# Mixer levels and softmax units interleaved on every engine, and 58 expert units instead of 56

## The chip, the cores and the metric

The kernel runs on one core of one Trainium2 chip. The metric is device time in microseconds (us); lower is better. Before the change three runs took 1692.69, 1696.32 and 1702.27 us, median 1696.32. The engines are named as in the profile: PE (TensorE, matmuls), DVE (VectorE), ACT (ScalarE), POOL (GpSimd) and SP (the queue that issues most loads).

## What is computed

One inference step of a two-layer trunk over 384 tokens (128 context, 256 latent; three tiles of 128), all in fp32, width 1024. Each layer has a modulated norm, one input projection, three mixers side by side (Fourier, differential attention, gated linear recurrence), an output projection, and a mixture of 64 experts with the best 8 for each token. Cut to the two mixers and the expert part that the change touches:

```python
# differential attention: 4 heads, two score maps a head
s = jnp.einsum('bqhmd,bkhmd->bmhqk', qblk, kf) * scale
p = jax.nn.softmax(s, axis=-1)
w = p[:, 0] - lam * p[:, 1]
o = jnp.einsum('bhqk,bkhd->bqhd', w, vf)

# recurrence (forward and backward), chunk by chunk
dec = jnp.where(causal, cum[:, :, :, None, :] - cum[:, :, None, :, :], -jnp.inf)
a = jnp.einsum('bhtk,bhsk,bhtsk->bhts', qc, kc, jnp.exp(dec))
o = o_inter + jnp.einsum('bhts,bhsv->bhtv', a, vc)

# experts: width 128, gates of the chosen 8
act = jax.nn.silu(hg) * hu * gates[:, :, None]
routed = jnp.einsum('tef,efd->td', act, p['w_down'])
```

## The kernel before

One program issues each engine's instructions in a fixed order written out by hand; the engines meet through semaphores. Within a layer the order is: modulation and norm, input projection (weights split into a high and a low part), Fourier mixer, recurrence, attention, output projection, router, experts, sum of the experts' rows.

**The recurrence in levels.** The pair matrix `aT` (source times target token, per tile and head) is filled by six levels (`NLEV`): four halvings of 64, 32, 16 and 8, and two last levels for the blocks of 8, forward and backward. For a level DVE takes differences of the summed log decays (`less_middle`, L1593, tile `diff` in `work`), ACT takes their exponentials (L1325, L1326; L1328, L1329 in the last two), DVE multiplies keys and queries with them (L1605, L1607; L1610, L1611), PE multiplies the two (L947, 12 products of 64 by 128, one for each tile, odd or even heads, and pair), and DVE copies the result under a mask into `aT` (`masked`, L1580). On DVE the products of level n come first, then the differences of n+1, then the masks of n-1. The levels' products go round all eight PSUM banks, six banks a level. After them: states (L957), the sum of the two halves of `aT` (L1624), the state copies, and the heads (L972, L976), which ACT takes out (L1336, L1337).

**The attention in units.** After the heads come twelve units, one for each tile and head, in a pipeline three deep on every engine. In step u, PE makes the two score maps of unit u (L990), turns the weights of unit u-2 (L998) and multiplies unit u-3 with the values (L1008); DVE takes the row maxima of unit u (L1646, L1648) and then makes the weights of unit u-1 (L1655 to L1660); ACT takes the exponentials of unit u (L1346), copies the turned weights of u-2 (L1353), and after a tile's last head copies the output and its squares (L1357, L1358). A unit of the first tile has 128 keys, the others 384. Scores and turned weights go round six banks, outputs use the other two. Then DVE sums the squares (L1670, L1671), ACT takes roots, DVE scales, and PE turns the rows (L1017). `prob`, `wts` and `wT` lie in the tile `h`, as do the sums `cum` and the keys `kkT` of the levels, so the attention can't start before the levels are done with them.

**Banks.** Every use of a bank is planned before: `banks.claim` makes PE wait until the use before it on the same bank was emptied, `banks.read` makes the reader wait until it was filled. A wait holds up all that stands behind it in its engine's order.

**Experts.** Tokens are packed into units of 128 rows, two windows of 64. A "whole" unit gives both windows to one of the busiest experts, a "pair" unit serves two experts, and a "spare" unit has windows for what overflows; the weights of a spare window are loaded only if it has an owner. With 56 units there are 16 whole, 24 pairs and 16 spare, in eight turns of "pair, whole, pair, spare, pair, whole, spare". Each load is one expert's 1.5 MB (3 x 512 KB). The 96 entries of the load list go round seven slots (`XSLOT`): SP waits for the unit that used the slot before, then issues; an entry without an owner keeps its slot. For each unit PE turns rows (L1129), makes gate and up products (L1143, 16 matmuls, 32 records), turns the activation (L1150) and makes the down products (L1158) of the unit before. POOL gathers and scatters the rows.

Of the kernel before, what the change touches and what calls it, by code (L numbers as in the profile page):

```python
# [18 lines left out]
ALU = mybir.AluOpType  # L19
# [3 lines left out]
P = 128  # L23
# [11 lines left out]
WIN = 64  # L35
NUNITS = 56
WHOLE = 16
PAIRED = 24
NXW = 32
# [110 lines left out]
def trunk_program(nc, T, CF, CM, y_prompt, y_sample, new_k, new_v, new_state):  # L150
# [22 lines left out]
    with ctx:  # L173
# [110 lines left out]
        prob = hflat[:, 0:4 * TOK].rearrange("p (a m t) -> p a m t", a=2, m=2)  # L284
        wts = hflat[:, 4 * TOK:6 * TOK].rearrange("p (a t) -> p a t", a=2)
        wT = hflat[:, 6 * TOK:8 * TOK].rearrange("p (a t) -> p a t", a=2)
        logf = mixer(NTILE, 2 * HW)
        att = logf
# [5 lines left out]
        att_sq = part(0, 4, DA)  # L294
# [86 lines left out]
        for stage, n in (("ada0", 2), ("ms1", 1), ("modT0", 2), ("ada1", 2), ("modT1", 2),  # L381
                         ("ada2", 2), ("q", DH), ("k", DH), ("modT2", 2), ("v", NTILE), ("fn", NTILE), ("hq", 2),
                         ("hif", NTILE), ("hbg", NTILE), ("k_rows", 1), ("ckT", 1), ("rotq", 2), ("rotk", 2),
                         ("four1", 4), ("zT", 2), ("fnT", 2), ("kkT", 4), ("cum", 4), ("past", 2), ("ada3", 2)):
            banks.plan("layer", stage, n)
        for use in range(2 * NTILE * NLEV):
            if use == 2 * NTILE:
                banks.plan("layer", "modT3", 2)
            banks.plan_one("layer", "lev", use, banks.turn % 8)
            banks.turn += 1  # L390
        for stage, n in (("st", 2), ("ho", 2)):
            banks.plan("layer", stage, n)
        UNITS = [(t, hd) for t in range(NTILE) for hd in range(DH)]
        NU = len(UNITS)
        ring6 = 0
        for u in range(NU + 3):
            if u < NU:
                for m in range(2):
                    banks.plan_one("layer", "sc", 2 * u + m, ring6 % 6)
                    ring6 += 1  # L400
            if 2 <= u < NU + 2:
                banks.plan_one("layer", "wT", u - 2, ring6 % 6)
                ring6 += 1
            if u >= 3 and UNITS[u - 3][1] == 0:
                banks.plan_one("layer", "o", UNITS[u - 3][0], 6 + UNITS[u - 3][0] % 2)
# [122 lines left out]
        for turn in range(8):  # L528
            for kind in ("pair", "whole", "pair", "spare", "pair", "whole", "spare"):
                u = UNITS_BY_KIND[kind].pop(0)  # L530
                owners = {"whole": [u], "pair": [u, u + PAIRED], "spare": [E + u - WHOLE - PAIRED, E + u - WHOLE - PAIRED + 16]}[kind]
                loads_of_unit.append([len(loads) + i for i in range(len(owners))] * (2 if kind == "whole" else 1))
                loads += [(len(order_of_units), w) for w in owners]
                order_of_units.append(u)
# [209 lines left out]
        def _(pe):  # L744
# [21 lines left out]
            for l in range(DEPTH):  # L766
# [169 lines left out]
                for n in range(NLEV):  # L936
                    if n == 1:
                        modulation_turned(3)
                    ka, qa = key_side[:, n % 2, :, :], query_side[:, n % 2, :, :]
                    pe.wait_ge(pair_ready.sem, pair_ready.at(l, n + 1))  # L940
                    for t in range(NTILE):
                        for odd in range(2):
                            use = (n * NTILE + t) * 2 + odd
                            bk = banks.claim(pe, "lev", use)
                            r = slice(HK * odd, HK * (odd + 1))
                            for c in range(2):
                                last = mm(bk[:, c * P:(c + 1) * P], ka[r, c, t * P:(t + 1) * P],  # L947
                                          qa[r, c, t * P:(t + 1) * P], start=True, stop=True)
                            banks.filled(last, "lev", use)


                pe.wait_ge(kdec_ready.sem, kdec_ready.at(l, 1))
                for i, tiles in enumerate(((0, 0), (1, 2))):
                    bk = banks.claim(pe, "st", i)
                    for d, t in enumerate(tiles):
                        for a in range(2):
                            last = mm(bk[:, (2 * d + a) * P:(2 * d + a + 1) * P], kdec[:, 2 * i + d, a * P:(a + 1) * P],  # L957
                                      hv[:, t, a * P:(a + 1) * P], start=True, stop=True)
# [992 lines left out]
```

## Time and profile before

| | us |
|---|---|
| runs, median of 3 | 1696.32 |
| profiled execution, its own time | 1706.42 |
| its span in the profile | 1704.6 |
| PE busy | 1406.1 (82%) |
| DVE busy | 671.4 (39%) |
| ACT busy | 408.3 (24%) |
| POOL busy | 256.3 (15%) |
| mean granted clock of PE | 0.881 |

The profile is that of one execution. Busy time is that of instructions of an engine; a share is over the whole span, whose stages have different limits. The granted clock is 1.0 at 2.4 GHz and 0.5 at 1.2 GHz; a stretch between them is a mix. Rows of a timeline give the start in us, the time taken in us, the engine and line, the operation, what it writes and reads, the number of instructions, and in brackets the idle time before it with what ended that. PE writes two records for each fp32 matmul.

### The profile page before, as it was taken

What the parts mean: (1) busy time and instruction counts of PE and PEld (TensorE: products, weight loads), DVE (VectorE), ACT (ScalarE), POOL (GpSimd) and SP (SyncE); (2) the same over time, 40 slices, a digit from 0 to 9 for tenths busy, and PEclk for the clock granted to TensorE, in tenths of its full rate; (3) what the DMA queues carried; (4) which work ended last, traced back from release to release, by engine and by line L of the source; (5) the groups of instructions that cost most, each with busy time, mean ns of one, the idle gap of its engine ahead of it and who ended that gap; (6) DMA issues with size and microseconds to landing.
All of it is one profiled execution on the core that took longest, in us unless ns stands there. A gap on an engine that the chain in (4) does not pass through costs nothing.

```text
span 1704.6 us, 23713 instructions
## 1 busy us (share of the span) xinstructions
PE 1406.1 (82%) x8772; PEld 962.6 (56%) x8772; DVE 671.4 (39%) x1382; ACT 408.3 (24%) x788; POOL 256.3 (15%) x273
## 2 busy tenths in 40 slices
PE   4799687986999999997059996888889999999942
PEld 2598465954555555554028875676655555555521
DVE  4422767153332222222743347633523222222246
ACT  2324425021222222221013344321112122222201
POOL 1000000001322222231010000000023232322200
PEclk9799857977999999999579996699889999999975
DMA  9553202126988888885874412122469888888853
GB/s 319 206 183 118 105 31 109 50 87 233 362 305 317 328 333 324 305 332 181 340 257 173 141 70 99 41 99 99 180 252 358 333 313 307 324 294 298 328 207 154
DMA packets 126098, 378.96 MB, mean 222 GB/s; under 512 B 28224, under 2 KB 33152, under 8 KB 122784
## 3 DMA queue, kind: packets, MB, share of 16 engines
q1 hardware_dynamic: 86976, 291.31, 46.2%
q0 software_dynamic: 35552, 60.97, 10.1%
q10 hardware_dynamic: 3456, 25.17, 3.6%
q8 instruction: 71, 1.16, 0.3%
q14 instruction: 43, 0.35, 0.1%
HBM read 480.36 MB, written 64.75 MB: 320 GB/s over the span
## 4 chain that ended last, share of the span: by engine, by line
PE 71%; DVE 16%; DMA 6%; issue 4%; ACT 2%; SPq 0%; DVEq 0%; ACTq 0%; POOLq 0%
PE bank L1143 25%; PE bank L1158 11%; PE bank L1129 7%; PE bank L1050 5%; PE bank L771 4%; PE bank L772 4%; PE bank L773 4%; DVE aT L1843 4%; DMA ring<-in_w_ada 3%; DVE aT L1580 1%; PE bank L1066 1%; DMA ring<-in_w_in 1%; PE bank L790 1%; PE bank L1114 1%; PE bank L976 1%
## 5 line engine op out<-in xcount | busy, mean ns | idle before, releaser
L1143 PE MATMUL bank<-slab,xT 128*64 128x256 f32 x2112 | 301.5, 396 | 20.6 <-issue 20.5
L1143 PEld LDWEIGHTS bank<-slab,xT 128*64 128x64 f32 x2112 | 180.6, 142 | 104.2 <-issue 38.2
L732 POOL DMA_INDIRECT sums_scratch<-h,row_table x112 | 112.8, 1007 | 538.6 <-PE bank L1129 438.4
L1826 DVE TENSOR_TENSOR work<-work,bank 128x128 f32<-128x128 f32 x112 | 32.3, 288 | 399.1 <-ACT work L1405 399.1
L1143 PE MATMUL bank<-ring,xT 128*64 128x256 f32 x960 | 152.7, 392 | 9.6 <-issue 9.6
L1158 PE MATMUL bank<-slab,work 128*64 128x512 f32 x528 | 147.3, 592 | 1.5 <-DVE work L1832 1.5
L1405 ACT ACTIVATE work<-bank 128x128 f32<-128x128 f32 x112 | 31.1, 278 | 457.5 <-PE bank L1143 457.5
L1815 DVE COPY h<-bank 128x512 f32<-128x512 f32 x112 | 77.5, 692 | 127.0 <-PE bank L1158 127.0
L1143 PEld LDWEIGHTS bank<-ring,xT 128*64 128x64 f32 x960 | 90.1, 140 | 44.8 <-issue 14.8
L1143 PE MATMUL bank<-h_hi_slot,xT 128*64 128x256 f32 x512 | 108.5, 396 | 6.4 <-issue 6.4
L1492 DVE TENSOR_TENSOR w_lo<-ring,w_hi 128x2048 fp32r<-128x2048 f32 x24 | 55.0, 2292 | 122.3 <-ACT w_hi L1229 122.3
L1129 PEld LDWEIGHTS bank<-consts,big 128*128 128x128 f32 x544 | 60.8, 145 | 68.3 <-issue 51.7
L1809 DVE COPY xT<-bank 128x512 f32<-128x512 f32 x112 | 77.5, 692 | 54.7 <-PE bank L1129 54.5
L1392 ACT ACTIVATE xT<-bank 128x512 f32<-128x512 f32 x112 | 67.1, 599 | 114.6 <-PE bank L1129 114.6
L1129 PE MATMUL bank<-consts,big 128*128 128x128 f32 x544 | 77.7, 288 | 16.0 <-DMA big<-rows_scratch,token_table 16.0
L1050 PE MATMUL bank<-big,ring 128*128 128x384 f32 x256 | 84.9, 488 | 0.0
L1179 PE MATMUL bank<-consts,aT 128*128 128x128 f32 x48 | 11.8, 428 | 88.4 <-DVEq L1846 88.4
L1398 ACT ACTIVATE h<-bank 128x512 f32<-128x512 f32 x112 | 67.0, 598 | 68.5 <-PE bank L1158 68.5
L725 POOL DMA_INDIRECT big<-rows_scratch,token_table x68 | 69.1, 1017 | 90.5 <-DVE token_table L1799 64.8
L1050 PEld LDWEIGHTS bank<-big,ring 128*128 128x128 f32 x256 | 80.1, 314 | 3.7 <-DVE mod L1464 0.2
L790 PE MATMUL bank<-ring,scond_wide 128*32 128x512 f32 x384 | 56.4, 724 | 29.8 <-DMA ring<-in_w_ada 29.8
L1229 ACT ACTIVATE w_hi<-ring 128x2048 fp32r<-128x2048 f32 x24 | 46.0, 1916 | 142.6 <-PE bank L773 87.6
(334 smaller groups left out, 2324.9 us busy)
## 6 DMA issues: line engine op xcount, KB each, us to landing
slab<-in_w_gate SPq DMA_DIRECT2D x112, 512.0 KB
slab<-in_w_up SPq DMA_DIRECT2D x112, 512.0 KB
slab<-in_w_down SPq DMA_DIRECT2D x112, 512.0 KB
ring<-in_w_ada SPq DMA_DIRECT2D x24, 2048.0 KB
ring<-in_w_gate SPq DMA_DIRECT2D x52, 512.0 KB
ring<-in_w_up SPq DMA_DIRECT2D x52, 512.0 KB
ring<-in_w_down SPq DMA_DIRECT2D x52, 512.0 KB
slab<-sums_scratch ACTq DMA_DIRECT2D x24, 1024.0 KB, 11.5
```

Source lines behind the costliest of these rows:

```text
L725: pool.indirect_dma_start(x_slots[n % XBUF], None, rows_dram, bass.IndirectOffsetOnAxis(ap=token_table[:, u:u + 1], axis=0), bounds_check= ...
L732: pool.indirect_dma_start(sums_dram, bass.IndirectOffsetOnAxis(ap=row_table[:, u:u + 1], axis=0), y_rows[:, n % 3, :], None, bounds_check= ...
L771: mm(out, a[0], b[0], start=start, stop=False)
L772: mm(out, a[0], b[1], start=False, stop=False)
L773: return mm(out, a[1], b[0], start=False, stop=stop)
L790: last = mm(bk[GROUP * ji:GROUP * (ji + 1), :], scond_wide[:, 4 * half + ji, :], w[:, ji, c * 512:(c + 1) * 512], start=(half == 0), stop= ...
L1050: last = mm(bk[:, 0:TOK], w[:, c, j:D:NJ], mixT[:, 4 * half + c, :], start=(half == 0 and c == 0), stop=(half == 1 and c == 3))
L1129: last = tr(bk[:, j * P:(j + 1) * P], x_slots[n % XBUF][:, (4 * half + j) * P:(4 * half + j + 1) * P], ident)
L1143: last = mm(bk[r, 0:2 * P].rearrange("p (k f) -> p k f", k=2), xT[:, n % 2, j, r], w[:, j, :, :], start=(j == 0), stop=(j == NJ - 1))
L1158: last = mm(bk[r, :], actT[:, n % 2, r], expert_slot(n, half)[0][:, 2 * D + c * 512:2 * D + (c + 1) * 512], start=True, stop=True)
L1809: banks.emptied(copy(xT[:, n % 2, 4:8, :].rearrange("p j s -> p (j s)"), bk[:, :]), "XTb")
L1815: banks.emptied(copy(y_rows[:, n % 3, 512:1024], bk[:, :]), "Yb")
```

## The change

The change does three things.

- **Order.** A list `STEPS` names levels, mask steps, units, states and heads in one order, and PE, ACT and DVE each run through it. Level 0 and its masks come first; from level 1 on there are two units to a level, one after `level` and one after `masks`; states, heads of tile 0, 1 and 2 are put between units 9 to 13. A level goes over PE in two parts: `level(n, 0)` covers tiles 0 and 1, `level(n, 1)`, in the mask step, covers tile 2. DVE does the second part's masks of level n-1 at the end of the level step, and the first part's masks of level n in the mask step.
- **Banks and memory.** Levels, states and heads have banks 6 and 7; scores 0 to 3; turned weights 4; outputs 5. `prob`, `wts` and `wT` move from `h` to the memory of `h_hi`, `att` and one tile of squares to that of `xT`. ACT sums each head's squares with `accum_out`, four instructions for each tile, and DVE's reduction of the attention's squares (L1670) goes.
- **Experts.** 58 units: 14 whole, 25 pairs, 19 spare; the load list has 102 entries. The order begins with "pair, whole, pair, pair, spare, pair" and is then dealt in proportion; the last is a spare. Written P, W, s it is: P W P P s P s W s W P s P W s P P s W P s W P s P P W s P s W P P s W P s P W s P P s W P s P W P s P W s P W s P s.

The diff, cut to its core:

```diff
-NUNITS = 56
-WHOLE = 16
-PAIRED = 24
-NXW = 32
+NUNITS = 58
+WHOLE = 14
+PAIRED = 25
+SPARE = NUNITS - WHOLE - PAIRED
+NXW = 2 * SPARE
...
-        prob = hflat[:, 0:4 * TOK].rearrange("p (a m t) -> p a m t", a=2, m=2)
+        prob = h_hi_slot[:, 0:4 * TOK].rearrange("p (a m t) -> p a m t", a=2, m=2)
...
-        att = logf
+        x_flat = xT[:, :, :, :].rearrange("p a j s -> p (a j s)")
+        att = x_flat[:, 0:NTILE * DA].rearrange("p (i f) -> p i f", i=NTILE)
+        att_sq = x_flat[:, NTILE * DA:NTILE * DA + DA]
...
+        banks.plan("layer", "ada3", 2, [0, 1])
+        banks.plan("layer", "modT3", 2, [2, 3])
+        banks.plan("layer", "lev", 4 * NLEV, [6, 7] * (2 * NLEV))
+        banks.plan("layer", "st", 2, [6, 7])
+        banks.plan("layer", "ho", 2, [6, 7])
...
+                    banks.plan_one("layer", "sc", 2 * u + m, 2 * (u % 2) + m)
...
+        LEVEL_PARTS = [((0, 1), 0), ((0, 1), 1), ((2,), 0), ((2,), 1)]
+        STEPS = [("level", 0), ("masks", 0), ("level", 1), ("unit", 0), ("masks", 1), ("unit", 1), ("level", 2), ("unit", 2),
+                 ("masks", 2), ("unit", 3), ("level", 3), ("unit", 4), ("masks", 3), ("unit", 5), ("level", 4), ("unit", 6),
+                 ("masks", 4), ("unit", 7), ("level", 5), ("unit", 8), ("masks", 5), ("unit", 9),
+                 ("states", 0), ("unit", 10), ("heads", 0), ("unit", 11), ("heads", 1), ("unit", 12), ("heads", 2),
+                 ("unit", 13), ("unit", 14)]
...
+        kinds = ["pair", "whole", "pair", "pair", "spare", "pair"]
+        total = {kind: len(units) for kind, units in UNITS_BY_KIND.items()}
+        while len(kinds) < NUNITS - 1:
+            late = {k: (total[k] - (k == "spare")) * (len(kinds) + 1) / (NUNITS - 1) - kinds.count(k) for k in total}
+            kinds.append(max((k for k in total if k != "spare" or kinds[-1] != k), key=late.get))
...
+                def level(n, part):
+
                     ka, qa = key_side[:, n % 2, :, :], query_side[:, n % 2, :, :]
                     pe.wait_ge(pair_ready.sem, pair_ready.at(l, n + 1))
...
+                    for k in (2 * part, 2 * part + 1):
+                        tiles, odd = LEVEL_PARTS[k]
+                        bk = banks.claim(pe, "lev", 4 * n + k)
+                        r = slice(HK * odd, HK * (odd + 1))
+                        for i, t in enumerate(tiles):
                             for c in range(2):
...
+                for what, k in STEPS:
+                    if what == "level":
+                        level(k, 0)
+                    elif what == "masks":
+                        level(k, 1)
+                        if k == 0:
+                            modulation_turned(3)
+                    elif what == "unit":
+                        unit(k)
+                    elif what == "states":
+                        states()
+                    else:
+                        heads(k)
...
+                        for hd in range(DH):
+                            cols = slice(hd * P, (hd + 1) * P)
+                            last = af(att_sq[:, cols], bk[:, cols], ACT.Square, accum_out=att_r[:, 0, t * DH + hd:t * DH + hd + 1])
+                        banks.emptied(last, "o", t)
...
+                for what, k in STEPS:
+                    if what == "level":
+                        level(k)
+                        if k == 0:
+                            rows_of_modulation(3)
+                    elif what == "unit":
+                        unit(k)
+                    elif what == "heads" and k == NTILE - 1:
+                        heads_taken()
...
+                        masked(n - 1, 1)
...
+                less_middle(0)
+                for what, k in STEPS:
+                    if what == "level":
+                        level(k)
+                    elif what == "masks":
+                        masked(k, 0)
+                        if k == 0:
+                            modulation(3)
+                    elif what == "unit":
+                        unit(k)
+                    elif what == "states":
+                        states()
...
-                red(att_r[:, 0, :], heads_a(att_sq), AX.X, ALU.add)
```

## Rows read from the trace of the kernel before

**Rows 1.** The head of the page.
```profile
span 1704.6 us, 23713 instructions
```

**Rows 2.** Busy time by stretch, all engines, granted clock, DMA share, GB/s.
```profile
195.00:236.00 41.00, 25.62 (x168) 22.52 (x168) 36.79 (x76) 11.41 (x22) 0.76 (x1) 0.54 0.23 92
236.00:251.00 15.00, 14.49 (x65) 12.80 (x66) 0.68 (x3) 1.29 (x4) 0.15 (x1) 0.56 0.04 9
251.00:283.00 32.00, 26.17 (x130) 17.14 (x131) 25.14 (x83) 19.37 (x67) 1.46 (x3) 0.73 0.14 50
404.00:805.00 401.00, 372.15 (x2744) 219.06 (x2744) 110.58 (x233) 82.63 (x168) 112.86 (x112) 0.97 0.82 301
1031.00:1072.00 41.00, 25.72 (x168) 22.61 (x168) 36.80 (x76) 11.41 (x22) 0.71 (x1) 0.54 0.23 92
```

**Rows 3.** The chain of waits, expert units of layer 0: start, us, what.
```profile
464.90 3.60 PE bank L1143 x32
...
474.86 6.21 PE bank L1143 x32
483.93 3.60 PE bank L1143 x32
490.38 3.60 PE bank L1143 x32
```

**Rows 4.** One expert unit's stretch: PE busy, clock, DMA share, GB/s.
```profile
459.65:466.10 6.45, 6.45 (x53) 1.00 1.03 413
```

**Rows 5.** The page's DMA queue of SP: packets, MB, share.
```profile
q1 hardware_dynamic: 86976, 291.31, 46.2%
```

**Rows 6.** Timeline of DVE, levels of layer 0.
```profile
195.29 1.82 DVE L1593 TENSOR_TENSOR work<-h 128x768 f32<-128x768 f32 x2
...
198.94 0.56 DVE L1605 TENSOR_TENSOR work<-h,work 128x384 f32<-128x384 f32 x1 [1.83 <-ACT work L1326]
...
208.42 2.09 DVE L1580 COPY_PREDICATED aT<-masks,bank 128x256 f32<-128x256 uint8 x6
...
232.30 1.76 DVE L1624 TENSOR_TENSOR aT<-aT 128x1536 f32<-128x1536 f32 x1
```

**Rows 7.** Timeline of DVE, the start of two attention units.
```profile
265.55 1.02 DVE L1646 TENSOR_REDUCE top<-bank 128x1 f32<-128x384 f32 x2
...
268.07 1.01 DVE L1646 TENSOR_REDUCE top<-bank 128x1 f32<-128x384 f32 x2
```

**Rows 8.** Timeline of ACT, one attention unit.
```profile
264.24 0.58 ACT L1346 ACTIVATE h<-bank,ntop 128x384 f32<-128x384 f32 x1 [1.30 <-DVE ntop L1648]
...
265.37 0.49 ACT L1353 ACTIVATE h<-bank 128x384 f32<-128x384 f32 x1
```

**Rows 9.** Timeline of PE, parts of attention units.
```profile
258.59 1.65 PE L990 MATMUL bank<-slab 64*128 64x384 f32 x4
...
263.02 0.87 PE L998 MATMUL bank<-consts,h 128*128 128x128 f32 x3
...
269.42 0.92 PE L990 MATMUL bank<-slab 64*128 64x384 f32 x4
...
278.77 1.49 PE L1008 MATMUL bank<-slab,h 128*128 128x128 f32 x6
...
280.69 2.16 PE L1008 MATMUL bank<-slab,h 128*128 128x128 f32 x12
```

**Rows 10.** Timeline of PE, the last level and the states.
```profile
228.18 3.09 PE L947 MATMUL bank<-work 64*128 64x128 f32 x24 [0.97 <-DVE work L1611]
231.20 3.50 PE L957 MATMUL bank<-slab 128*128 128x128 f32 x16
```

**Rows 11.** Timeline of PE, two quarters of the heads.
```profile
238.00 0.69 PE L972 MATMUL bank<-slab,aT 128*128 128x64 f32 x2
...
239.67 0.69 PE L972 MATMUL bank<-slab,aT 128*128 128x64 f32 x2
```

**Rows 12.** Timeline of DVE, the attention's squares.
```profile
284.16 1.75 DVE L1670 TENSOR_REDUCE att_r<-work 128x12 f32<-128x1536 f32 x1 [4.48 <-ACT work L1358]
```

More of the change, by code:

```diff
@@ L293, in trunk_program @@
         four1 = part(0, 4)
-        att_sq = part(0, 4, DA)
         zT = part(4, 6)
@@ L946, in _ @@
                             for c in range(2):
-                                last = mm(bk[:, c * P:(c + 1) * P], ka[r, c, t * P:(t + 1) * P],
+                                last = mm(bk[:, (2 * i + c) * P:(2 * i + c + 1) * P], ka[r, c, t * P:(t + 1) * P],
                                           qa[r, c, t * P:(t + 1) * P], start=True, stop=True)
[L949 to L958, printed above, removed]
-                    banks.filled(last, "st", i)
@@ new lines, in heads @@
+                def heads(t):
+                    if t == 0:
+                        pe.wait_ge(qdec_ready.sem, qdec_ready.at(l, 1))
+                        pe.wait_ge(pairs_summed.sem, pairs_summed.at(l, 1))
+                        banks.wait_emptied(pe, "st", 1)
+                    for odd in range(2):
+                        if t == 0:
+                            banks.claim(pe, "ho", odd)
+                        bk = banks.banks[banks.uses["layer"]["ho", odd][0]]
+                        r = slice(HK * odd, HK * (odd + 1))
@@ L977, in _, with unit @@
                                               start=False, stop=(d == 1))
-                    banks.filled(last, "ho", odd)
-                pe.wait_ge(rope_done.sem, rope_done.at(l, 1))
-                banks.wait_emptied(pe, "ckT")
-                for u in range(NU + 3):
+                        if t == NTILE - 1:
+                            banks.filled(last, "ho", odd)
+                def unit(u):
+                    if u == 0:
+                        pe.wait_ge(rope_done.sem, rope_done.at(l, 1))
+                        banks.wait_emptied(pe, "ckT")
                     if u < NU:
@@ L1312, in _, with level @@
                 af(lam_s[:, :], lam_s[:, :], ACT.Exp).then_inc(lam_exp.sem, 1)
-                for n in range(NLEV):
-                    if n == 2:
-                        rows_of_modulation(3)
+                def level(n):
                     act_e.wait_ge(diff_ready.sem, diff_ready.at(l, n + 1))
@@ L1594, in less_middle, with level @@
                     last.then_inc(diff_ready.sem, 1)
-                less_middle(0)
-                for n in range(NLEV):
+                def level(n):
                     dve.wait_ge(fac_ready.sem, fac_ready.at(l, n + 1))
```

136 lines of the change are left out of this document (60 added, 76 removed).

## Prediction

> **What bounds the kernel now.** I read the page's head first [rows 1]: the profiled execution spans 1704.6 us and took 1706.4, 10 above the median of 1696.3, so the sum is made as a difference and added to both. Then the table of stretches [rows 2]. The reader is to see two different limits. In the mixer levels (195 to 236 us, and 1031 to 1072 in the second layer) DVE is busy 36.8 of 41 us and PE runs at a granted 0.54. In the heads of the mixer (236 to 251) DVE has nothing: 0.68 of 15. In the attention (251 to 283) DVE is busy 25.1 of 32. In the expert loop PE is busy 372 of 401. The part that the change interleaves goes from the first difference at 195.3 to the end of the last attention product at 280.69 + 2.16 = 282.85 [rows 6, 9]: 87.5 us, of which DVE is idle some 25. That idle time is the most that interleaving can win in a layer; the expert units are a separate matter.
>
> **Part 1: two more expert units.** The chain of waits shows a unit every 6.45 us: 483.93 to 490.38 [rows 3]. Two more, in two layers, are 4 x 6.45 = 25.8 us if nothing gives way. Something may: in each turn of seven units one waits for its weights, here from 471.4 to 474.86, and its matmuls take 6.21 instead of 3.60 at a lower clock. From 464.90 to 483.93 two units took 19.03 instead of 12.9, so 6.1 were lost. I walked the old load list by the code's rule (load i waits until the unit of load i-7 is done, skipped spare loads hold a slot all the same): the waits fall on units 9, 16, 23, 30, 37, 44, 51, the third unit of a turn, and 9 is where the trace has it. The bound is the slots, not the DMA engines, which carry 413 GB/s in one stretch of 6.45 us [rows 4] and 301 over the loop. No spare load ran before: the 291.31 MB of the queue [rows 5] are the dense weights and 128 experts. The new list still has 64 real loads, but puts two pairs side by side. The same walk gives it waits at units 5, 16, 25, 32, 41 and 48: six, not seven, four of them 1.5 us longer (two pairs after each other need four loads in 12.9 us). 4 x 1.5 more and one wait of about 3.7 less: about nothing, or 2 us less for shorter slow spells. So 11 to 13 us a layer; I take 12, **+24 us in all**, with 16 and 32 as ends. The wider one-hot tables (58 columns for 56) cost under 0.1 us on DVE and I count nothing.
>
> **Part 2: the interleaving.** What each engine does stays nearly the same; the order changes, and with it the handoffs. Durations before: on DVE a level is four products (198.94 to 200.9, 1.95 us), two differences (1.83) and six masked copies (2.09, 0.35 each) [rows 6]; a wait of 1.83 for ACT's exponentials shows what those take; the sum of the masks is done at 232.30 + 1.76 = 234.1. Old order: the masks of level n-1 cover the exponentials of n+1, and eight banks let PE run ahead. A later softmax unit costs 2.52 us on DVE (265.55 to 268.07) [rows 7]; a unit of the first tile, with a third of the keys, I put at 1.6 (an estimate). On ACT it is two exponentials (0.58) and a copy (0.49, of which 0.4 until the next can start) [rows 8]. On PE its scores take 1.65 us at the half clock and 0.92 at full, its transposes 0.87, its product 1.49 (1.3 to the next start) [rows 9]. A level's 24 matmul records take 3.09 at the half clock; the states take 3.50 [rows 10].
>
> New order, walked through the list of steps. The levels have two banks, so a level goes over PE in two parts: 16 records (3.09 x 16/24 = 2.1 us), and 8 (1.1). A part can't start before DVE has emptied both banks, and PE takes steps in order, so the scores of the next unit stand queued behind that part. Three handoffs follow, each on the path.
> (a) Level, then unit. DVE ends its level step with the last two masked copies of the level before. Only then does PE start the first part, 2.1, and then the scores, 1.65. The two halves of the rows overlap by some 0.45 (an estimate: the 24 records of rows 10, 0.43 us each, fit into 3.09 because both halves run together), and DVE waits 3.3 us; 2.5 for the first tile, whose scores are a third as wide. Twice 2.5 and three times 3.3 (levels 1 to 5): 14.9.
> (b) Masks, then unit. The second part and the scores: 1.1 + 1.65 - 0.65 = 2.1 (the first bank is free one mask earlier); 1.4 for the first tile. Two and three of these: 9.1.
> (c) Unit, then level. ACT takes the exponentials of the level in the same place of the list, behind those of the unit: 1.15 + 0.4 + 1.8, while DVE has 1.4 us of its own: 1.9 us of waiting, 1.6 for the first tile. Levels 2 to 5: 7.3.
> At the start DVE waits 1.8 for the first exponentials, and for the rows of modulation 3, which PE turns after the second part of level 0: 0.3 + 3.0. In total 36.4 us of waits. To them come DVE's own works up to the sum of the masks: 34.5 of the levels (36.8 less the 2.3 of the states) and 20 of the units 0 to 9 (four at 1.6, six at 2.52, less the last half). Together 90.9, where the trace has 234.1 - 195.3 = 38.8.
>
> **The end of it.** From there PE is the bound, at the half clock: wait for the states 1.5; units 10 and 11 at 1.65 + 0.87 + 1.3 = 3.8 each; heads of tile 0, 1.0; heads of tiles 1 and 2, each 4 x 1.66 = 6.64 (239.67 less 238.00 is one of four quarters [rows 11]); after each the transposes and product of an old unit, 2.2; last product 1.5. Sum 29.3. So the last attention product ends 90.9 + 29.3 = 120.2 us after the start, against 87.5: **+32.7 a layer**. Heads and units of PE don't overlap, they follow each other, and the idle time of DVE under the heads comes back at another place. The squares of the attention are now summed on ACT: DVE's reduction of 1.75 us goes [rows 12], ACT takes four small squares instead of one large, about 0.8 more: -1.0 a layer, on the path to the norm. The walk in the old order, with the same durations, ends at 284.8 where the trace has 282.8, so it is good to some 2 us in 88. The moved tiles (probabilities and attention rows in free memory) add no wait that I find. SP's and POOL's queues keep their order: the shared expert's weights wait for the heads, and the weight blocks of the next modulation for PE, 32 us later but with the same time ahead of them. **+31.7 x 2 = +63**.
>
> **The clock.** PE idles 5 and 2.5 us in each cycle of the new order and is busy for about 60% of it, as in the old levels (25.6 of 41), which ran at 0.54 [rows 2]. So I take half rate. In the last 29 us PE is nearly without a gap; there the old heads, busy 14.5 of 15 us, had 0.56, but the attention after them rose to full during the second tile. The Trainium skill, TensorE: Matmul & The Clock Gate, Part 1: The HAM clock gate, says that the default state is throttled and that sustained activity releases it; by that alone the end would run at 2.4 GHz, and the sum would be 4 to 6 us less a layer. The trace speaks against it for the heads. I keep half rate and put full rate into the range.
>
> **Sum.** +24 + 63 = +87. 1706.4 + 87 = 1793 for an execution like the profiled one, **1783 us** against the median.
>
> **Rivals.**
> R1, PE granted the full clock (17%). Then (a) becomes 1.2 + 0.92 - 0.4 = 1.7 and (b) 1.2, waits fall by some 13 us, and the end from 29.3 to 23.4: +13 a layer, 26 + 24 = +50, **1746**. For it: attention at full rate from 265 us. Against: the gaps.
> R2, it becomes faster (7%). PE's products for DVE are always there, and DVE is the bound: 62.2 us of work from rows 2, start 1.8, modulation 3.3 and 5 of drain = 72 against 87.5, -16.5 a layer with the saved reduction: -33 + 24 = -9, **1687**, -0.5%. It decides if (a) and (b) stay under 0.3 us each. Against: four banks for the scores don't help when they are queued behind a blocked level part.
> R3, the new spare units are free (8%), because they fill the waits for loads: +63 alone, **1759**. Against: two units add slots' worth of time only where there is a wait, and the pairs side by side eat that.
> R4, the interleaving does nothing (8%): waits won under the heads equal those lost: +24, **1720**.
> R5, about nil by half of R2's gain (5%): **1698**.
> My forecast: 55%, its own range 1768 to 1800.
>
> **How the numbers follow.** Faster by over 0.5% (8.5 us, about what a measurement of this kernel can tell): R2, 0.07. Within: R5, 0.05. Slower: 0.88. The range reaches from R1 and below it (some full clock with cheap units) to the forecast with dearer loads: 1728 to 1806; R2, R4 and R5 stay out.
>
> **What would show it.** In the profile after: DVE's reductions of a unit waiting for PE's scores, 2 to 3 us, behind each level and each mask step; level products waiting for ACT near 1.9; the sum of the masks about 91 us behind the first difference and the last attention product about 120; granted clock near 0.55; 58 units of 6.45 and six or so waits. If the sum of the masks comes within 70, R2's side is right, and the place of PE's scores in the queue was read wrongly.

## The result and the profile after

The changed kernel takes **1813.09 us**, median of three runs (1812.61 to 1814.11), against 1696.32 before: ratio **1.0685** [1.0635, 1.0734], +116.8 us. The direction was forecast; the time lies 30 us above the predicted 1783 and 7 above the range. The head of the page of the changed kernel, its shares of busy time and SP's queue (packets, MB, share), which answer to [rows 1] and [rows 5]:

```profile
span 1812.3 us, 24367 instructions
...
PE 1456.2 (80%) x8968; PEld 1001.7 (55%) x8968; DVE 679.4 (37%) x1396; ACT 416.3 (23%) x842; POOL 263.6 (15%) x281
...
q1 hardware_dynamic: 86976, 291.31, 43.5%
```

The loads are the same to the byte. This execution took 1814.11 us and stands 1 us above its median, where the profiled one of before stood 10 above its own. So two traces put side by side show 107.7 us, and the medians 116.8.

Where they went, by stretches cut at the same instructions in both traces (us; layer 0 / layer 1):

| stretch | before | after |
|---|---|---|
| first difference to first matmul of the output projection ("mixer") | 101.2 / 98.9 | 132.4 / 133.7 |
| output projection to the router's table | 105.5 / 104.7 | 106.2 / 105.3 |
| table to the first gate/up matmul | 12.4 / 11.8 | 13.8 / 13.6 |
| first to last gate/up matmul ("loop") | 382.3 / 386.0 | 404.1 / 402.2 |
| last gate/up matmul to the new x | 61.5 / 52.7 | 60.9 / 53.2 |

The mixers take 66.0 us of the 107.7, the loops 38.0, the table's way to the experts 3.2. Nothing else moved by more than 0.7.

Windows of the changed kernel (bounds, length, busy time of PE, PEld, DVE, ACT, POOL, granted clock, DMA share, GB/s), to be read against [rows 2]:

```profile
195.00:290.00 95.00, 51.08 (x252) 41.19 (x254) 56.10 (x139) 25.24 (x79) 0.00 (x0) 0.57 0.10 40
290.00:316.00 26.00, 23.92 (x118) 19.08 (x122) 8.12 (x23) 9.01 (x35) 2.37 (x4) 0.68 0.16 53
447.00:849.00 402.00, 377.04 (x2787) 223.32 (x2787) 111.42 (x236) 83.14 (x170) 107.84 (x107) 0.97 0.79 288
1085.00:1179.00 94.00, 49.73 (x239) 39.87 (x240) 55.08 (x138) 25.24 (x79) 0.00 (x0) 0.55 0.11 42
```

In the first and the last row no engine is busy for even 60% of the time: DVE has 56 of 95 us, PE 51, ACT 25. Before, DVE had 36.8 of 41 in the levels. So in the interleaved stretch no engine is the bound; they wait for each other. The timeline of DVE shows how (start, us, line, operation, and in brackets the idle time before it and its releaser):

```profile
258.55 0.76 DVE L1624 COPY_PREDICATED aT<-masks,bank 128x256 f32<-128x256 uint8 x2
262.82 1.25 DVE L1686 TENSOR_REDUCE top<-bank 128x1 f32<-128x384 f32 x2 [3.51 <-PE bank L1005]
...
265.57 1.42 DVE L1624 COPY_PREDICATED aT<-masks,bank 128x256 f32<-128x256 uint8 x4
268.98 1.16 DVE L1686 TENSOR_REDUCE top<-bank 128x1 f32<-128x384 f32 x2 [1.99 <-PE bank L1005]
...
273.63 0.96 DVE L1654 TENSOR_TENSOR work<-slab,work 128x768 f32<-128x768 f32 x1 [1.91 <-ACT work L1358]
...
288.15 1.76 DVE L1669 TENSOR_TENSOR aT<-aT 128x1536 f32<-128x1536 f32 x1
...
316.10 0.95 DVE L1724 TENSOR_REDUCE ho_r<-big 128x12 f32<-128x768 f32 x1 [16.97 <-ACT xT L1391]
```

One cycle has the three handoffs of the prediction (each is a wait of one engine for what another has to finish first): after the level's masks 3.51 us for the scores, after the next masks 1.99 for the scores, then 1.91 for ACT's exponentials. The sum of the masks starts at 288.15, 93.0 us after the first difference (37.0 before [rows 6]). The last row is DVE idle for 16.97 us under the heads and the last units: the idle time of the heads has moved, not gone. PE in the same cycle, and at the end:

```profile
259.13 2.42 PE L955 MATMUL bank<-work 64*128 64x128 f32 x13 [6.34 <-DVE aT L1624]
261.14 1.00 PE L1005 MATMUL bank<-slab 64*128 64x384 f32 x1
261.35 0.84 PE L955 MATMUL bank<-work 64*128 64x128 f32 x3
261.94 1.53 PE L1005 MATMUL bank<-slab 64*128 64x384 f32 x3
...
266.48 1.36 PE L955 MATMUL bank<-work 64*128 64x128 f32 x6 [1.75 <-DVE aT L1624]
...
297.26 0.33 PE L985 MATMUL bank<-slab,aT 128*128 128x64 f32 x2
...
298.11 0.43 PE L985 MATMUL bank<-slab,aT 128*128 128x64 f32 x2
...
309.13 0.69 PE L985 MATMUL bank<-slab,aT 128*128 128x64 f32 x2
...
311.49 2.76 PE L1024 MATMUL bank<-slab,h_hi_slot 128*128 128x128 f32 x12
```

PE stands idle for 6.34 us although the scores of the next unit (L1005) have all they need: they are queued behind the level's products (L955), which wait for DVE's masks. The last attention product ends at 314.25, 119.1 us after the start.

In the expert loop, PE's waits (total, number, longest), of the kernel before from 415 to 800 us and of the changed one from 447 to 850:

```profile
PE bank L1143 <- issue: 18.2, 7, 3.5
```
```profile
PE bank L1173 <- issue: 25.0, 10, 5.3
```

Seven waits for weights became ten. The chain of waits of the changed kernel shows the longest, at unit 16 of layer 0 (start, us, what):

```profile
545.41 3.60 PE bank L1173 x32
551.86 5.34 issue
557.20 6.01 PE bank L1173 x32
566.06 3.60 PE bank L1173 x32
572.51 3.60 PE bank L1173 x32
```

The wait costs 5.34, and the unit's products run 6.01 instead of 3.60, so the next one starts 2.4 us late too. Without waits a unit starts 6.45 us behind the one before. In layer 0 the starts lie further apart at units 5 (by 1.8), 16 (5.4), 19 (1.5), 25 (3.2), 28 (1.0), 32 (4.0), 35 (1.4), 41 (3.1), 44 (1.5) and 48 (2.9), and at the unit right behind five of them (by 1.7 to 2.3).

### The profile page after: what moved, and what is told of

It is laid out like the page before. It is cut to its first block, busy times and chain, and to the rows that moved or that the text cites. A ratio compares the mean times of both kernels' runs of the same rounds, so it can differ in the third digit from the quotient of the medians.

```text
span 1812.3 us, 24367 instructions
## 1 busy us (share of the span) xinstructions
PE 1456.2 (80%) x8968; PEld 1001.7 (55%) x8968; DVE 679.4 (37%) x1396; ACT 416.3 (23%) x842; POOL 263.6 (15%) x281
## 4 chain that ended last, share of the span: by engine, by line
PE 72%; DVE 14%; DMA 6%; issue 4%; ACT 3%; SPq 0%; DVEq 0%; POOL 0%; POOLq 0%; ACTq 0%
PE bank L1173 24%; PE bank L1188 11%; PE bank L1159 7%; PE bank L1080 5%; PE bank L780 4%; PE bank L782 4%; PE bank L781 4%; DVE aT L1896 3%; PE bank L955 3%; DMA ring<-in_w_ada 3%; PE bank L1005 1%; PE bank L1096 1%; DMA ring<-in_w_in 1%; PE bank L799 1%; DMA big<-rows_scratch,token_table 1%
## 5 line engine op out<-in xcount | busy, mean ns | idle before, releaser
L1173 PE MATMUL bank<-slab,xT 128*64 128x256 f32 x2016 | 260.9, 404 | 43.5 <-issue 43.5
L1173 PEld LDWEIGHTS bank<-slab,xT 128*64 128x64 f32 x2016 | 161.8, 145 | 124.5 <-issue 60.5
L1173 PE MATMUL bank<-ring,xT 128*64 128x256 f32 x992 | 124.9, 382 | 5.7 <-issue 5.7
L955 PE MATMUL bank<-work 64*128 64x128 f32 x288 | 57.8, 433 | 86.7 <-DVE aT L1624 72.9
L1188 PE MATMUL bank<-slab,work 128*64 128x512 f32 x504 | 124.7, 593 | 1.5 <-DVE work L1885 1.5
L955 PEld LDWEIGHTS bank<-work 64*128 64x128 f32 x288 | 51.4, 315 | 94.7 <-issue 69.7
L1173 PE MATMUL bank<-h_hi_slot,xT 128*64 128x256 f32 x704 | 102.8, 382 | 0.2 <-issue 0.2
L1862 DVE COPY xT<-bank 128x512 f32<-128x512 f32 x116 | 80.2, 691 | 59.4 <-PE bank L1159 59.1
L1159 PE MATMUL bank<-consts,big 128*128 128x128 f32 x576 | 82.2, 288 | 19.2 <-DMA big<-rows_scratch,token_table 19.2
L1173 PEld LDWEIGHTS bank<-ring,xT 128*64 128x64 f32 x992 | 76.1, 137 | 37.3 <-issue 10.6
L734 POOL DMA_INDIRECT big<-rows_scratch,token_table x72 | 73.0, 1014 | 92.0 <-DVE token_table L1852 63.1
L1209 PE MATMUL bank<-consts,aT 128*128 128x128 f32 x48 | 11.8, 426 | 88.3 <-DVEq L1899 88.3
```

Of the source, the lines that this page charges most:

```text
L734: pool.indirect_dma_start(x_slots[n % XBUF], None, rows_dram, bass.IndirectOffsetOnAxis(ap=token_table[:, u:u + 1], axis=0), bounds_check= ...
L955: last = mm(bk[:, (2 * i + c) * P:(2 * i + c + 1) * P], ka[r, c, t * P:(t + 1) * P], qa[r, c, t * P:(t + 1) * P], start=True, stop=True)
L1159: last = tr(bk[:, j * P:(j + 1) * P], x_slots[n % XBUF][:, (4 * half + j) * P:(4 * half + j + 1) * P], ident)
L1173: last = mm(bk[r, 0:2 * P].rearrange("p (k f) -> p k f", k=2), xT[:, n % 2, j, r], w[:, j, :, :], start=(j == 0), stop=(j == NJ - 1))
L1188: last = mm(bk[r, :], actT[:, n % 2, r], expert_slot(n, half)[0][:, 2 * D + c * 512:2 * D + (c + 1) * 512], start=True, stop=True)
L1862: banks.emptied(copy(xT[:, n % 2, 4:8, :].rearrange("p j s -> p (j s)"), bk[:, :]), "XTb")
```

## The experiments

**Theory.** The mixers lose time because PE and ACT take their steps in DVE's order: work that is ready stands behind work that waits for DVE. The loops lose it to the two units and to the *order* of the load list. **Rivals:** the clock, PSUM banks or DVE's own instructions in the mixers; in the loops the mere number of spare entries, or the rate of the DMA engines. All kernels were measured beside the kernel before. In the table the mixer and loop columns are from one trace each.

| kernel | ratio [95%] | median us | masks' sum starts after | mixer L0 / L1 | loop L0 / L1 |
|---|---|---|---|---|---|
| after | 1.0685 [1.0635, 1.0734] | 1813.1 | 93.0 | 132.4 / 133.7 | 404.1 / 402.2 |
| units58 | 1.0306 [1.0257, 1.0355] | 1747.3 | 37.0 | 100.5 / 101.1 | 404.0 / 403.7 |
| mix56 | 1.0316 [1.0265, 1.0368] | 1754.8 | 92.3 | 131.9 / 131.1 | 385.7 / 381.3 |
| mix56_scores | 1.0194 [1.0143, 1.0246] | 1730.1 | 74.4 | 115.9 / 115.9 | 371.9 / 382.1 |
| mix56_act | 1.0278 [1.0242, 1.0314] | 1748.0 | 85.9 | 127.0 / 126.7 | 384.1 / 379.5 |
| mix56_both | 1.0060 [1.0029, 1.0090] | 1705.9 | 65.2 | 106.7 / 107.5 | 382.9 / 382.0 |
| mix56_more | 0.9991 [0.9969, 1.0014] | 1695.9 | 65.4 | 101.8 / 101.2 | 376.9 / 377.3 |
| dealt56 | 0.9964 [0.9938, 0.9990] | 1690.4 | 37.0 | 101.1 / 100.5 | 380.2 / 378.1 |
| walk56 | 0.9984 [0.9958, 1.0009] | 1693.9 | 37.0 | 101.0 / 98.9 | 387.4 / 376.8 |
| walk58 | 1.0073 [1.0049, 1.0096] | 1706.4 | 37.0 | 100.5 / 98.9 | 381.2 / 387.0 |
| heads | 0.9913 [0.9884, 0.9941] | 1684.1 | 37.0 | 94.7 / 95.0 | 386.2 / 381.2 |
| heads_dealt56 | 0.9909 [0.9884, 0.9934] | 1682.4 | 37.0 | 94.7 / 96.9 | 381.5 / 377.6 |

### The two halves of the change apart

**units58** is the kernel before with the units and their order of the change; **mix56** is the changed kernel with the 56 units of before, so its edit is the reverse of that of units58, which is:

```diff
-NUNITS = 56
-WHOLE = 16
-PAIRED = 24
+NUNITS = 58
+WHOLE = 14
+PAIRED = 25
...
-        for turn in range(8):
-            for kind in ("pair", "whole", "pair", "spare", "pair", "whole", "spare"):
+        kinds = ["pair", "whole", "pair", "pair", "spare", "pair"]
...
```

> The kernel before with the change's expert part alone: 58 units (14 whole, 25 pairs, 19 spare) in the new order; mixers and attention as before. My forecast had +24 us. The theory after the result (the new load order adds small waits at units 19, 28, 35 and 44 that my walk with shorter load times did not show, and the seven real loads at the start delay the first gather) says +41: 38 in the two loops and 3 before them. If the expert loop costs more only because it follows the new mixers, this run stays near +24.

> The change's interleaving alone, with the 56 units, their counts and their order as before. My forecast had +63; the two traces put +66 on this part. If both parts are independent, the excess of this run and that of units58 add up to that of the changed kernel, 107 to 117.

units58 cost +3.06%, mix56 +3.16%; together 6.2, the change 6.85 [6.35, 7.34]. In medians it is 51.9 and 59.4 us, together 111, within the 107 to 117 expected. Each half is known to 0.5%, so within the noise they add up, and neither hides the other. The loops of units58 (404.0, 403.7) are those of the changed kernel, and its mixers are those of before. By medians units58 is +52 us, where the theory said 41 and the forecast 24. By loops it is less: fourteen loops of the old order, from this table and the kernel before, lie between 371.9 and 386.2 with a mean of 381.4; four of the new one between 402.2 and 404.1, mean 403.5. That is **+22 a layer**, of which two units of 6.45 are 12.9. PE's waits in one loop of units58, from 430 to 850 us:

```profile
PE bank L1149 <- issue: 25.0, 10, 4.6
```

Ten waits again. mix56 has DVE's waits of the changed kernel to within 0.5 us: 24.2 for the scores there, the other three rows alike (from 194 to 320 us: total, number, longest):

```profile
DVE top L1681 <- PE bank L1000: 23.7, 12, 3.5
...
DVE work L1644 <- ACT work L1350: 5.0, 3, 1.8
DVE work L1649 <- ACT work L1353: 3.6, 2, 1.9
DVE mod L1503 <- PE bank L808: 3.0, 2, 2.4
```

### PE: the scores ahead of what waits for DVE

In **mix56_scores** PE issues the scores of a unit ahead of the level part, states or heads that stand in front of it. No instruction is added.

```diff
-                for what, k in STEPS:
+                for at, (what, k) in enumerate(STEPS):
+                    if what == "unit":
+                        if STEPS[at - 1][0] == "unit":
+                            scores(k)
+                    elif STEPS[at + 1][0] == "unit":
+                        scores(STEPS[at + 1][1])
```

> As mix56, but PE issues the scores of the next unit ahead of the level part (or states, or heads) that stands before that unit in the list; nothing else moves, no work is added or removed. Theory one (the handoff: scores queued behind a level part that waits for DVE's masks): DVE's waits of 3.5 and 2.0 us for scores go, 19 us a layer, so about 38 us less than mix56. Theory two (PE's total work at the half clock is the bound, wherever it stands): within 6 us of mix56.

```profile
DVE mod L1511 <- PE bank L808: 6.2, 4, 2.5
DVE top L1689 <- PE bank L1000: 5.1, 4, 1.9
DVE work L1652 <- ACT work L1358: 5.0, 3, 1.8
DVE work L1657 <- ACT work L1361: 3.6, 2, 1.9
DVE aT L1627 <- PE bank L950: 2.7, 6, 1.4
```

The wait for the scores falls from 23.7 to 5.1 us, the sum of the masks starts 17.9 earlier, and the mixers lose 16.0 and 15.2, together 31; the medians differ by 25. Expected were 38. The masks now wait a little for their own products (2.7 instead of 0.5), as they should when the scores go first. (Two of the four waits for the modulation belong to the next stage, which now lies in the window; in the levels they are 2.36 and 0.66 as before.) The granted clock rose too, from 0.56 to 0.64 (195.6 to 271), so a faster PE is a rival. The first part of the stretch tells them apart, since it ran at the half clock throughout (a stretch with its clock of 0.50, and the last reduction of the first tile):

```profile
197.60:231.50 33.90, 20.41 (x104) 17.60 (x104) 22.83 (x61) 10.75 (x35) 0.00 (x0) 0.50 0.22 87
```
```profile
228.69 0.49 DVE L1689 TENSOR_REDUCE top<-bank 128x1 f32<-128x128 f32 x2 [0.35 <-PE bank L1000]
```

There the four reductions of the first tile wait 0.35 us in all instead of 8.6 in the changed kernel, and the last of them starts 33.1 us after the first difference instead of 39.7: the same matmuls in another order do that without the clock. In the rest of the stretch, at 0.74, what the order gives and what the clock gives aren't told apart.

### ACT: the exponentials ahead of the unit's

**mix56_act** lets ACT take the exponentials of levels 2 to 5 one step earlier; **mix56_both** is that on top of mix56_scores.

```diff
+                act_steps = list(STEPS)
+                for n in range(2, NLEV):
+                    at = act_steps.index(("level", n))
+                    act_steps.insert(at - 1, act_steps.pop(at))
-                for what, k in STEPS:
+                for what, k in act_steps:
```

> As mix56, but ACT takes the exponentials of levels 2 to 5 one unit earlier; PE's order stays the change's. Theory one (each handoff is a wait of its own on DVE's path, so they add): 8 us a layer less than mix56, 16 in all, as between mix56_scores and mix56_both. If the wait for ACT is only the shadow of the wait for PE, it gives nothing without the other edit.

> As mix56_scores, and ACT takes the exponentials of levels 2 to 5 one unit earlier in its order. Theory one: the waits of 1.6 to 1.9 us of DVE for ACT at four levels go, 8 us a layer, so about 54 us less than mix56, and still some 10 us above the kernel before, because the end of the mixers (states, heads, last units) stays PE's. Theory two: within 10 us of mix56.

DVE's waits, of mix56_act and then of mix56_both:

```profile
DVE top L1685 <- PE bank L1000: 24.2, 11, 3.5
...
DVE work L1648 <- ACT work L1350: 1.8, 1, 1.8
```
```profile
DVE top L1693 <- PE bank L1000: 3.1, 3, 1.6
DVE aT L1631 <- PE bank L950: 2.7, 6, 1.4
DVE work L1656 <- ACT work L1358: 1.8, 1, 1.8
```

In both only the first level's exponentials are still waited for; the four later waits, 6.8 us, are gone. Alone this gives 4.9 and 4.4 us a mixer, less than the 8 that I expected: the sum of the masks comes 6.4 earlier, but the end is PE's and gives 1.5 of it back. On top of the scores it gives 9.2 and 8.4, and the median of mix56_both is 49 us below that of mix56, of 54 expected. So the two waits shadow each other a little, and together they carry **25.2 and 23.6 of the 30.7 and 32.2 us** that interleaving had cost: (a) to (c) were the main cause. The banks and DVE's own instructions are the same in mix56_both as in mix56, so these two rivals have at most the 5.5 and 8.6 us that are left. mix56_both is still 0.6% slower than before, with a sum of the masks at 65.2.

### What is left: heads in pairs, modulation later

**mix56_more** adds two things: it puts the products of odd and even heads of the same tile next to each other, and lets modulation 3 come one step later on PE and DVE. **heads** is the first of these alone, on the kernel before.

```diff
-                    bk = banks.claim(pe, "ho", odd)
-                    r = slice(HK * odd, HK * (odd + 1))
-                    for t in range(NTILE):
-                        for c in range(2):
+                    banks.claim(pe, "ho", odd)
...
+                for t in range(NTILE):
...
+                    for c in range(2):
+                        for odd in range(2):
...
+                        if t > 0:
+                            for d in range(2):
+                                src = state0 if (t == 1) == (d == 0) else st_mid
+                                for odd in range(2):
+                                    r = slice(HK * odd, HK * (odd + 1))
+                                    last[odd] = mm(outs[odd][c], qdec[r, 2 * d + c, t * P:(t + 1) * P], src[r, 2 * d + c, :],
+                                                   start=False, stop=(d == 1))
```

> As mix56_both, with the heads' products grouped as in the run heads, and modulation 3 turned on PE after the first part of level 1 and taken by DVE ahead of the masks of level 1. Expected: 5 us a layer less for the heads and 2 to 3 us for modulation 3, for which DVE waited 2.4 us in level 0: about 15 us less than mix56_both, the mixers at 99 us a layer against 101 before: near the kernel before, within 0.5%. If PE's work at half the clock is by now the bound of the whole stretch, only the heads' 5 us a layer come.

> The kernel before, with the products of the mixer's heads in another order on PE: for each tile and pair, the products of odd and even heads stand next to each other (two banks, two halves of the rows), so that the products with 64 rows can run side by side. Same products, nothing added. Theory one (a quarter of 1.66 us is four 64-row records after each other and two changes between 128 and 64 rows): 3.3 us less a layer, 6 to 7 in all. Theory two (weight loads or the granted clock of about 0.55 set the pace of the heads): no change. In either case the whole time lies under 0.5% from before, so the trace's heads stretch decides.

The timeline of PE in heads, one pair of quarters, where [rows 11] had two of 1.67 one after the other:

```profile
238.47 1.11 PE L973 MATMUL bank<-slab,aT 128*128 128x64 f32 x4
239.51 0.69 PE L980 MATMUL bank<-state,big 64*128 64x64 f32 x4
240.00 0.64 PE L980 MATMUL bank<-st_mid,big 64*128 64x64 f32 x4
240.57 1.11 PE L973 MATMUL bank<-slab,aT 128*128 128x64 f32 x4
```

A pair takes 2.10 us, against 2 x 1.67 = 3.34. The products over 128 rows cost a little less (1.04 to the next start for four records, where two had 0.62): 0.2 of the 1.24 us. Those over 64 rows, one head on rows 0 to 63 and the other on 64 to 127, now start 0.49 and 0.57 us apart for four records, as before for two: they run side by side, which is the other 1.04. The records are as long as before (0.69, 0.64), at a granted 0.57 against 0.56, so it isn't the clock. The Trainium skill, TensorE: Matmul & The Clock Gate, Part 3: Packing small matmuls, says that products with few rows run at the same time when they lie in different row groups of the array; the trace agrees, for fp32 and two groups. heads gained 0.87% [0.59, 1.16], more than the 0.5% expected, with mixers 6.5 and 3.9 us shorter; the four pairs of a layer make 5.0. The mixers of mix56_more are 4.9 and 6.3 shorter than those of mix56_both, and its median is 10 us lower, of 15 expected. The later modulation has no share in this that shows: the sum of the masks starts no earlier (65.4 after 65.2), since the wait only moved and grew (3.0 to 4.0 together):

```profile
212.10 0.19 DVE L1519 TENSOR_REDUCE mod<-bank 128x8 f32<-128x32 f32 x1 [3.38 <-PE bank L808]
212.95 0.19 DVE L1519 TENSOR_REDUCE mod<-bank 128x8 f32<-128x32 f32 x1 [0.66 <-PE bank L808]
```

With all of it, interleaving has a mixer of 101.5 where the order of before, with heads in pairs, has 95. On this kernel it doesn't pay even when its handoffs are mended.

### The order of the load list

Three orders, each a string of P (pair), W (whole) and s (spare), in the diff in this order. **dealt56**: the kernel before, its own 16, 24 and 16 units dealt by the rule of the change. **walk56** and **walk58**: orders that a walk of the load list rated best, with one fixed time for a load; walk58 has the 14, 25 and 19 units of the change.

```diff
-        for turn in range(8):
-            for kind in ("pair", "whole", "pair", "spare", "pair", "whole", "spare"):
+        for kind in 'PWPPsPWsWsPWPsPWsPWPsPWsPWPsPWPsWPsPWPsWPsPWPsWPPsWPsWPs':
+        for kind in 'PWPPPsWPsWPWsPPsWPsPWWsPPsPsWPWsPPWWsPPsWPsPWWsPPWWsPPss':
+        for kind in 'PPPWPWsPPssPsPWsWWPsPWPsPWWsPPsPsWPsPsWPWsPPsWPWsPsPsWPsPs':
```

> The kernel before (56 units, its counts, its mixers), with its units in the order that the change's dealing rule gives for them: P W P P s P W s W s P W P s P W s and so on. Theory S (the waits come from which unit frees a slot for which load, so the order of the units sets them, and the number of units costs 6.45 us each): my walk of the load list gives 10 us less a layer than the old order, so about 20 us less than before. Theory D (the DMA engines are the bound of the loop, order does not matter): within 5 us of before.

> As dealt56, with an order chosen by walking the load list so that few units wait: P W P P P s W P s W P W s P P s W P s P W W s P P s P s W P W s P P W W s P P s W P s P W W s P P W W s P P s s. Theory S: 20 to 26 us less a layer than the old order, 40 to 50 us less than before in all. Theory D: within 5 us of before.

> The kernel before with the change's counts (58 units: 14, 25, 19), in an order walked in the same way. Theory S: two units more cost 12.9 us a layer but the waits fall by more, so 5 us less a layer than the kernel before, about 10 less in all, and some 55 us less than units58, which has the same counts. If the number of units, or the larger tables, were the cost: near units58, 40 to 50 above before.

(In the order of the change as it is written out ahead of the prediction, units 21 and 22 are exchanged: the rule deals a pair and then a whole.) dealt56 was expected 20 us faster and gave 6 (0.36%, [0.10, 0.62]). walk56 was expected 40 or more faster and gave nothing that can be measured; in its layer 0 the starts lie too far apart at units 7 (2.1 us), 14 (4.3), 17 (3.2), 33 (3.2) and 41 (3.8), among others. So the walk with one fixed load time rates orders wrongly, and that theory fell. These two runs alone would fit the rival, the rate of the DMA engines, nearly as well: it said within 5 us of before. walk58 decides. It was expected 10 us faster than before and took 9 to 12 more (1.0073), but against units58, with the same units, spare entries and loads in another order, it is 1706.4 to 1747.3. So neither the number of spare entries nor the engines' rate alone sets the time of units58. PE's waits of walk58 from 415 to 800 us, and its busy row from 414.5 to 795.5:

```profile
PE bank L1144 <- issue: 10.6, 6, 3.3
```
```profile
414.50:795.50 381.00, 370.42 (x2807) 218.40 (x2805) 110.97 (x235) 82.92 (x170) 108.80 (x108) 1.00 0.82 301
```

Six waits of 10.6 us instead of ten of 25.0, and the granted clock rounds to 1.00 for the stretch: one unit is slow behind a wait, unit 11 with 5.36. The engines moved 301 GB/s, where the loop of the change had 288. With 58 units the two loops take 384.1 in the mean, 2.7 more than with 56; the order of the change makes that 22.1. **The two more units cost some 3 us a layer in a good order; the order of the change costs the other 19.** The 3 is rough: it rests on loops of 381.2 and 387.0, and by the medians the whole kernel is 9 to 12 us slower than before, 4 to 6 a layer. Each unit still takes its 6.45; what walk58 saves is waits. Which property makes an order good stays open: not the number of waits that my walk counts.

### A kernel faster than both

**heads_dealt56** joins heads and dealt56, with the edits shown.

> The two edits that gained, together, on the kernel before: heads grouped, and its 56 units in the order of dealt56. They touch different stages, so the gains should add: 0.87% and 0.36%, together 1.2%, about 1677 us; faster than both kernels.

0.9909 [0.9884, 0.9934], 1682.4 us, where 1677 was expected: faster than both kernels, by the paired heads. What dealt56 had shown, 6 us, doesn't show on top of heads' 0.9913; loops of one order spread by up to 14 us, and 6 us is near what can be told.

## Why the prediction was right, and where it failed

**Part 2, the interleaving: right, with two misses that cancel.** Forecast +31.7 a layer; the traces show +31.2 and +34.8 (the mixers of before differ by 2.3 between the layers, those after by 1.3 the other way). Point by point in layer 0:

| | forecast | measured |
|---|---|---|
| (a) level, then unit: first tile / later | 2.5 / 3.3, sum 14.9 | 2.96 / 3.51, sum 16.5 |
| (b) masks, then unit | 1.4 / 2.1, sum 9.1 | 1.35 / 2.00, the last 1.01, sum 7.7 |
| (c) unit, then level | 1.6 / 1.9, sum 7.3 | 1.54 / 1.91, sum 6.7 |
| start and modulation | 5.1 | 1.83 + 3.02 |
| all waits of DVE up to the masks' sum | 36.4 | 36.3 |
| DVE's own work up to there | 54.5 | 58.4 |
| masks' sum done | 90.9 | 94.7 |
| from there to the last attention product | 29.3 | 24.3 |
| last attention product | 120.2 | 119.1 |

The waits include 0.5 of the masks for their own bank. The forecast's sum of (c) should be 7.0: two of the four levels follow a unit of the first tile. DVE's own work was 3.9 short, 2.2 of it in the units: one of the first tile takes about 1.8, not my 1.6, and a pair of reductions 1.15 to 1.25 instead of the 1.02 of [rows 7], which goes with scores that come one by one: in mix56_scores, where they are ready, it is 1.01 again. The end was 5 too long: the granted clock was 0.68 there, and the first quarters of the heads start 0.85 us apart before they fall back to 1.66. That is R1's end (23.4), without R1's waits. The saving in the squares was 0.3, not 1.0. The level stretch had 0.57 granted, as forecast.

**R2 fell, and its own test shows why.** I had written that a masks' sum within 70 us would prove R2's side right. mix56_both has it at 65.2, and the mixer is still 5.5 us longer than before. R2 took DVE as the bound and gave 5 us to drain; but behind the masks' sum come states, heads and the last units, nearly all on PE (busy 25.9 of 29 us at a granted 0.65), and in mix56_both the last attention product ends at 93.4, 28 us after the sum of the masks starts, against 87.6 before. Units that are already done can't fill the idle time behind that point.

**Part 1, the experts: the failed step.** The forecast was +12 a layer with 16 as the end; measured +22 in the mean of loops (38.0 for both in the two profiled traces). The units themselves, 12.9, were right. The step that failed is the walk of the load list, "about nothing, or 2 us less". Measured are 9 us more in place of its nothing. It had named units 5, 16, 25, 32, 41 and 48, and at all six there is a wait; in layer 0 they cost 20.4 us, where the seven of before cost 18.7, close to the walk's 2.3 more. But it missed the waits at 19, 28, 35 and 44 (5.3 together), and it counted on 2 us less for slow spells, that is units at a lower clock behind a wait, which were 1.6 more (9.1 after 7.5). In layer 1 the missed four cost 5.0, and the slow spells were 3.6 less than those of the profiled execution of before. PE's waits rose from 18.2 to 25.0. The walk gave each load one time; that this was too simple, walk56 showed. What sets the time of a load, and so the four waits, stays open. Also "the bound is the slots, not the DMA engines" was taken from one stretch at 413 GB/s [rows 4]: it shows what the engines can move for 6.45 us, not what seven loads get when they start together.

**The sum.** Against the profiled execution the forecast was 1793 and the changed one took 1814.11: 21 short, 14 of it in the loops (38.0 for 24), 3 in the mixers (66.0 for 63), 3 on the way from the table to the experts, which I hadn't costed. Against the medians it is 30, because the profiled execution of before was 10 above its median, its loops 1 and 5 us above the mean of their order, and I took 10 off the forecast for that; its loops were then also my base for a difference that is nearer to 44 than to 38. A range of 16 to 32 for the experts was too narrow at the top: 44 lay outside. With 32 in its place the time would have been 1801, within the 1806 of the range.

## What to carry to other kernels

When two streams of work are laid into one order that several engines run through, ask for each engine separately what stands behind a waiting step: here the same list for PE, ACT and DVE cost 31 us a layer, and moving the scores ahead of the step that blocked them gave half of it back; on this kernel the old order, with the heads in pairs, stayed the faster one. Here interleaving could fill idle time only of an engine that was idle *and* had work whose inputs were ready; the idle time of DVE under the heads was 14 us before and 17 after. And where loads pass through a few slots, treat the order of their users as a size to be measured: one order against another moved some 40 us with not a byte or a matmul changed.

## What the runs showed of the hardware

- Two fp32 products over 64 rows, on rows 0 to 63 and 64 to 127, ran side by side once they were neighbours in PE's order, and not while each half's products stood together: a pair of quarters of the heads fell from 3.34 to 2.10 us, 0.87% of the kernel for a reordering.
- In the level stretches PE was granted 0.55 to 0.57 while busy 51 of 95 us; in the heads of before 0.56 while busy 14.5 of 15 [rows 2]; from 297 to 299 us of the changed kernel the same quarters ran at nearly twice the pace (0.85 us apart), behind a stretch of larger products. Why the one spell had the full clock and the other not, no run here tells.
- The same loop of 56 units in the same order took from 371.9 to 386.2 us in fourteen loops of seven traces, with the seven main waits at the same units but of different length. The loop of the change's order, with more waits, spread less (402.2 to 404.1 in four loops of two traces).
